# Eight modulation chunks of layer 0 move from TensorE products to VectorE dot products; attention weighs its values one head later

## The reference

```python
mod_l = split((silu(c) @ ada_w[i] + ada_b[i])[:, None, :], N_MOD)      # 6 rows of 1024
mod_c = split((silu(c_ctx) @ ada_w[i] + ada_b[i])[None, None, :], N_MOD)
a_l = modulate(rms_norm(x, norm1_w[i]), mod_l[0], mod_l[1])            # x * (1 + scale) + shift
...
q, k, v = project(a)            # low-rank latents, RMS norms, rotary part; 8 heads
o_l = softmax(q_l @ k_all.T * scale) @ v_all ; o_c = softmax(q_c @ k_c.T * scale) @ v_c
x = x + mod_l[2] * (o_l @ w_o)
x = x + mod_l[5] * swiglu(modulate(rms_norm(x, norm2_w[i]), mod_l[3], mod_l[4]), w1, w3, w2)
```

## Time and profile before

| | |
|---|---|
| median of three runs | 2816.22 us |
| profiled execution, its own time | 2820.6 us |
| its span | 2818.8 us |
| PE busy | 2587.3 us (92%) |
| PEld busy | 1440.2 us (51%) |
| DVE busy | 1079.4 us (38%) |
| ACT busy | 650.4 us (23%) |
| mean granted TensorE clock | 0.972 |
| DMA moved | 664.83 MB |

### The profile page before, as it was taken

How to read it: one execution, slowest core, us unless ns; L and a number is a source line. 1 busy time by engine, 2 the same in 40 slices (tenths; PEclk the granted TensorE clock), 3 DMA queues, 4 the chain that set the end, 5 groups by cost and what they waited for, 6 DMA issues and landing times. The chain is left out here.

```text
span 2818.8 us, 32353 instructions
## 1 busy us (share of the span) xinstructions
PE 2587.3 (92%) x12008; PEld 1440.2 (51%) x12008; DVE 1079.4 (38%) x2410; ACT 650.4 (23%) x1255; POOL 28.4 (1%) x34
## 2 busy tenths in 40 slices
PE   7999999999999998999989899999989999777776
PEld 3555544444477667888654533333347765222222
DVE  2432487771046665772431522222143323010112
ACT  2343200000055553100243312122122222111011
POOL 0000000000000000000000000000010000000000
PEclk9999999999999999999999999999999999888888
DMA  6133455562222212875301799999953338999997
GB/s 265 77 122 118 179 225 234 234 244 75 97 98 75 75 46 75 311 299 194 118 15 72 312 403 421 422 422 421 421 219 126 135 112 359 421 422 422 422 422 304
DMA packets 104137, 664.83 MB, mean 236 GB/s; under 512 B 12585, under 2 KB 21033, under 8 KB 27376
## 3 DMA queue, kind: packets, MB, share of 16 engines
q1 hardware_dynamic: 98720, 651.26, 58.0%
q0 software_dynamic: 3600, 6.07, 0.6%
q10 hardware_dynamic: 1728, 6.29, 0.6%
HBM read 663.27 MB, written 7.34 MB: 238 GB/s over the span
## 5 line engine op out<-in xcount | busy, mean ns | idle before, releaser
L699 PE MATMUL PB<-A,RING 128*128 128x256 f32 (+1 forms) x1440 | 454.6, 479 | 2.4 <-ACT A L570 2.4
L699 PEld LDWEIGHTS PB<-A,RING 128*128 128x128 f32 x1440 | 273.4, 190 | 184.1 <-issue 160.2
L447 DVE SCALAR_TENSOR_TENSOR WORK<-RING,MORE 128x1024 f32<-128x1024 f32 x288 | 335.5, 1221 | 20.2 <-ACT MORE L713 11.2
L510 PE MATMUL PB<-BIG,RING 128*128 (+2 forms) x928 | 310.7, 497 | 5.6 <-PEq L664 3.3
L510 PEld LDWEIGHTS PB<-BIG,RING 128*128 128x128 f32 x928 | 175.9, 190 | 139.4 <-issue 128.7
L2552 DVE TENSOR_TENSOR BIG<-BIG,PB 64x512 f32<-64x512 f32 x32 | 22.1, 690 | 352.2 <-ACT BIG L2449 352.2
L3051 DVE TENSOR_TENSOR BIG<-BIG,PB 64x512 f32<-64x512 f32 x16 | 11.0, 690 | 372.7 <-ACT BIG L2969 372.7
L585 DVE SCALAR_TENSOR_TENSOR X<-PB,MODS,X 128x256 f32<-128x256 f32 x72 | 32.5, 480 | 298.0 <-PE PB L539 297.2
L2869 PE MATMUL PB<-RING,X 128*32 128x512 f32 x384 | 100.6, 770 | 40.6 <-DMA RING<-moe_w 40.6
L718 ACT ACTIVATE RS<-PB 128x512 f32<-128x512 f32 (+1 forms) x44 | 21.6, 491 | 414.8 <-PE PB L699 414.8
L1715 PE MATMUL PB<-A,RING 128*128 128x512 f32 x224 | 98.3, 592 | 0.0
(11 more groups left out here) (495 smaller groups left out, 3881.6 us busy)
## 6 DMA issues: line engine op xcount, KB each, us to landing
RING<-moe_w SPq DMA_DIRECT2D x144, 1024.0 KB
RING<-ada_rows SPq DMA_DIRECT2D x72, 1024.0 KB
RING<-ffn_w SPq DMA_DIRECT2D x66, 1024.0 KB
SPARE<-moe_w SPq DMA_DIRECT2D x48, 1024.0 KB, 24.1
MORE<-moe_w SPq DMA_DIRECT2D x48, 1024.0 KB, 24.9
A<-moe_w SPq DMA_DIRECT2D x40, 1024.0 KB
BIG<-moe_w SPq DMA_DIRECT2D x36, 1024.0 KB, 26.6
CST<-moe_w SPq DMA_DIRECT2D x24, 1024.0 KB
```

The source lines that it names most:

```text
L447: dve_.scalar_tensor_tensor(out=JUNK[:, n % 4, :], in0=RING[:, s, b * D:(b + 1) * D], scalar=1.0, in1=WIDE[:, side // 2, w, :], op0=ALU.mu ...
L510: last = pe_.matmul(PB[:, m, 0:tp], tile(s, 2, D)[:, r, m * P:(m + 1) * P], src(2 * i + r), start=first and r == 0, stop=False)
L699: last = pe_.matmul(PB[:, 2 * s + j, x], tile(s, KD, P, j * KD * P)[:, k, :], A[:, k, x], start=k == 0, stop=k == KD - 1)
```

## The change

Layer 0's chunks 4 to 11 are no longer computed by TensorE. All are dot products on VectorE, laid out by column like those of the other layers, in four places:
- chunks 4 and 5 in the latents stage of `mla`: four DMAs into `BIG` at the block's start, four dots after each token tile's norms (the first four ahead of them). The spread vectors (`WIDE_0`, in SPARE) are loaded at the end of `opening` in place of head weights and late constants, which SP now issues in `mla`, behind those four DMAs.
- chunks 6 and 7 in the heads stage: two dots a head, between the maxima and the shares.
- chunks 8 and 9 in the attention's output product (`side_dots` with `sides=(0, 0)`).
- chunks 10 and 11 in the output product of layer 0's feed-forward, behind the 16 dots that are there; their weights go to SPARE, A and SIL, 1.5 MB issued at the end of the feed-forward and 2.5 MB at the start of the product, ahead of SP's first load there.

In the heads stage TensorE's list is now: scores of h+1, flips of h, values of h-1. ScalarE copies the flipped scores of h, then makes the exponentials of h+1, then copies the result of h-1. Two warming products stand ahead of the last head's values. In every boundary VectorE waits for its last bias sum before GAIN.

```diff
-    def opening(latent_weights, head_weights):
+    WIDE_0 = SPARE[:, 1, :].rearrange("p (w k) -> p w k", w=2)
+    DOTS = SMALL[:, 0:16].rearrange("p (j n) -> p j n", j=2)
+
+    def gate_dot(dve, of, n, source, wide, junk):
+        m, b = n % 8, len(junk)
+        if n >= b:
+            dve.wait_ge(*of("dotted", n - b + 1))
+        dve_.scalar_tensor_tensor(out=junk[n % b], in0=source, scalar=1.0, in1=wide[:, m % 2, :], op0=ALU.mult,
+                                  op1=ALU.mult, accum_out=DOTS[:, n // 8 % 2, m:m + 1]).then_inc(sig("dotted").sem, 1)
+
+    def gate_add(dve, of, n, chunk):
+        dve.wait_ge(*of("dotted", n + 1))
+        dve_.tensor_tensor(MODS[:, 0, 4 * chunk:4 * chunk + 4, :], DOTS[:, n // 8 % 2, :].rearrange("p (n w) -> p n w", w=2),
+                           ada_bias(0, 4 * chunk, 4), ALU.add).then_inc(sig("mod_added").sem, 1)
...
                     latent_weights(sp, j)
-                head_weights(sp)
-                sp.dma_start(CST[:, late:CON["decay"][0]], io["consts_late"]).then_inc(sig("late_in").sem, 16)
-                sp.dma_start(SPARE[:, 0, 0:2 * 7 * HD], io["decay"]).then_inc(sig("late_in").sem, 16)
+                sp.dma_start(WIDE_0.rearrange("p w k -> p (w k)"), io["cwide"][0]).then_inc(sig("wide_in").sem, 16)
...
             elif product:
+                if gates:
+                    for n in range(2):
+                        sp.dma_start(GATE_TILES[1 + n], ada_of(0)[10 + n, 1 - n]).then_inc(loaded[7 + n].sem, 16)
+                    sp.dma_start(GATE_TILES[4], ada_of(0)[11, 1, :, D:2 * D]).then_inc(loaded[9].sem, 16)
                 with sp.Fori(0, pairs) as i:
...
             for share in side_shares(sides):
-                side_dots(dve, of, sides, share, 0, 11)
+                side_dots(dve, of, sides, share, 0, chunks)
+            added = len(sides)
+            if gates:
...
+                for n in range(16):
+                    if n % 4 == 0:
+                        dve.wait_ge(*of(f"loaded{6 + n // 4}", 32 if n == 12 else 16))
+                    gate_dot(dve, later, n, halves[n // 2], WIDE[:, 0], [JUNK[:, b, :] for b in range(4)])
+                    if n % 8 == 7:
+                        gate_add(dve, later, n, 10 + n // 8)
+                added += 2
+            if added:
+                dve.wait_ge(*of("mod_added", added))
...
             def _(sp):
+                for n in range(4):
+                    sp.dma_start(BIG[:, n * SLOT:(n + 1) * SLOT], ada_of(0)[4 + n // 2, n % 2]).then_inc(loaded[6 + n].sem, 16)
+                mla_heads(sp)
...
-                def side_products(h):
-                    if h:
-                        pe.wait_ge(sig("mod_added").sem, sig("mod_added").at(h))
...
                 scores(0)
                 for h in range(HEADS):
+                    if h:
+                        pe.wait_ge(sig("turned").sem, sig("turned").at(2 * h))
                     if h + 1 < HEADS:
                         scores(h + 1)
                     flips(h)
-                    side_products(h)
-                    weigh(h)
-                    side_flips(h)
+                    if h:
+                        weigh(h - 1)
+                keep_warm(7, 2)
+                weigh(HEADS - 1)
...
             def _(act):
+                act.wait_ge(sig("wide_in").sem, sig("wide_in").at(16))
+                act_.activation(WIDE_0, WIDE_0, ACT.Silu).then_inc(sig("wide_silued").sem, 1)
+                act_.activation(SMALL[:, 250:251], con("eps"), ACT.Sqrt)
...
+                act.wait_ge(*of("dotted", 16))
                 for u in range(units):
...
+                dve.wait_ge(sig("wide_silued").sem, sig("wide_silued").at(1))
+                latent_dots(0)
                 for t in range(NT):
...
+                    if t < 3:
+                        latent_dots(t + 1)
...
-                    if h:
-                        dve.wait_ge(sig("mod_flipped").sem, sig("mod_flipped").at(h))
...
+                    for w in range(2):
+                        gate_dot(dve, of, n + w, RING[:, s, h % 2 * D:h % 2 * D + D], WIDE_0, HEAD_JUNK)
                     for j in range(2):
                         dve.wait_ge(sig("exped").sem, sig("exped").at(2 * h + j + 1))
```

More of the change, by code:

```diff
@@ L433, in side_shares, with side_dots @@
         return spots[:len(sides)], spots[len(sides):]
-    def side_dots(dve, of, sides, share, i, chunk):
+    def side_dots(dve, of, sides, share, i, chunks):
         dots = 8 * len(sides)
@@ L453, in side_dots @@
             if x == 1:
+                chunk = chunks[j]
                 dve_.tensor_tensor(MODS[:, side, bass.ds(4 * chunk, 4), :],
@@ L456, in side_dots, with boundary @@
                                    ada_bias(side, 4 * chunk, 4), ALU.add).then_inc(sig("mod_added").sem, 1)
-    def boundary(product, gain, layer, shift, scale, t, free, rest, sides=(), begun=False):
+    def boundary(product, gain, layer, shift, scale, t, free, rest, sides=(), begun=False, chunks=(11, 11), gates=False):
         at = {name: signal.base for name, signal in signals.items()}
@@ L614, in boundary @@
             loaded[s].passed(16)
-        passed(mod_added=len(sides), dotted=8 * len(sides))
+        passed(mod_added=len(sides) + 2 * gates, dotted=8 * (len(sides) + 2 * gates))
+        for n in range(4 if gates else 0):
+            loaded[6 + n].passed(32 if n == 3 else 16)
         for s in range(2 if product and not begun else 0):
@@ L725, in _ @@
                     for s in range(2):
[L726 removed]
+                        side_dots(dve, of, sides, shares[s], i, (i, i))
                         dve.wait_ge(sig("silu_made").sem, sig("silu_made").at(2 * i + s + 1))
@@ L808, in mla @@
         PTB = [w for w in (WORK[:, 3 * T:6 * T], AF[:, 3 * T:6 * T])]
-        ROW = WORK[:, 6 * T:8 * T].rearrange("p (b t) -> p b t", b=2)
+        HEAD_SPOTS = (3, 2, 4, 5)
+        LATENT_JUNK = [MORE[:, b * D:(b + 1) * D] for b in (2, 3)]
+        HEAD_JUNK = [RING[:, 1, b * D:(b + 1) * D] for b in range(2)]
         def latent(t):
@@ L1026, in _, with exps @@
                 unit_out(units - 1)
-                for h in range(HEADS):
+                def exps(h):
                     bank, b = 3 * (h % 2), h % 2
@@ L1060, in _, with latent_dots @@
                 chain(last)
+                def latent_dots(tile):
+                    dve.wait_ge(*of(f"loaded{6 + tile}", 16))
+                    for m in range(4):
+                        at = tile * SLOT + m // 2 * D
+                        gate_dot(dve, of, 4 * tile + m, BIG[:, at:at + D], WIDE_0, LATENT_JUNK)
+                    if tile % 2:
+                        gate_add(dve, of, 4 * tile + 3, 4 + tile // 2)
+                dve.wait_ge(sig("wide_silued").sem, sig("wide_silued").at(1))
+                latent_dots(0)
                 for t in range(NT):
@@ L1156, in mla @@
         for s in (2, 3, 4, 5):
-            used[s].passed(HEADS // 2)
-            loaded[s].passed(16 * HEADS // 2)
+            used[s].passed(1)
+            loaded[s].passed(16)
+        for n in range(4):
+            loaded[6 + n].passed(16)
         n = HEADS
```

104 lines of the change are left out of this document (61 added, 43 removed).

## The result

The changed kernel takes **2795.27 us**, the median of 6 executions (2793.55 to 2797.03), against 2815.95 for the kernel before beside it (6 executions, 2815.04 to 2818.84). The ratio is 0.9927, interval 0.9917 to 0.9937, and the gain 20.7 us. The forecast was 2794.5.

A forecast was written before the change was run, and what follows sets the result against it. TensorE's own work was taken to bound seven of eight heads. Attention's output product starting 22.2 us earlier, other places free, took 2816.2 to 2794.0; plus 0.5 for the clock gave 2794.5, eight-in-ten range 2791 to 2802.

The forecast's parts named there:

- TensorE's list bounds the heads, and what leaves it is gained: Heads stage: TensorE is busy 86.10 of 86.10 us; eight chunk products and flips, 21.4 us, leave its list.
- The replayed chain: Heads: ScalarE's copies have 1.5 us to spare, VectorE's shares 3.8; new waits only at head 2's scores and the last head.
- The head's length: Heads: 12.28 us less 2.67 for chunk products and flips leaves 9.61 us of TensorE a head, for six heads.
- The clock term: Whole kernel: 0.5 us added to 2794.0 for possible stretches at the 1.2 GHz level.
- The first rival: Heads: the clock falls at the new short waits, costing 1.7 to 3.4 us; 2796 to 2797.5 if once; chance 22%.
- One aside of the prediction: Heads: 2.8 us of the gain is the old last head's slow clock and wait, offset by new waits and warming products.
- The sum of 22.2: Attention's output product starts at 241.13 in place of 263.29, a difference of 22.2 us, taken as the whole gain.
- The dots cost nothing: Heads: two dots at a pace of 1.15 us each stay under the chain by 0.6 us, so no cost.
- The upper bound of 1.7: Heads: if dots take twice the pace, 2.3 us each, only the last head's wait grows, by 1.7 us.
- The 0.6 us to spare: Heads: VectorE's dots have been over for 0.6 us when its reciprocal is wanted, at s + 9.5.
- The latents cost nothing: Latents: 4.6 us of dots before each reciprocal fit VectorE's idle time; moved DMAs no cost, bounds 0 and +1.
- The second weight tile is in time by 1.9 us: Feed-forward's output product: 6.3 MB at 430 GB/s take 14.6 us, landing at 640.5 against 642.40 wanted; no wait.

The follow-up runs named there:

- the short ones: Changed kernel with all 64 dot products of layer 0's eight chunks cut from 1024 columns to 32; 2794.05 us, ratio 0.9917.

## Why the prediction was right

- **TensorE's list bounds the heads, and what leaves it is gained.** Right. The replayed chain held too: ScalarE's copies and VectorE's shares were in time in all heads but the first and last, with waits of 1.16 (forecast 1.27) and 1.12 (1.04). The experiment that puts the values back shows that this had to be argued: without the later values the same list takes 9.3 us more.
- **The head's length was mis-sized**, 9.61 against 9.33. The 12.28 less the chunk products and flips takes what is left of a head to be as long as before. From start to start it is shorter: flips 1.36 for 1.46, values 2.59 for 2.69 (the row at 181.00 is 1.89 long where the earlier trace rows have 1.99), scores 5.38 for 5.46, 0.28 in all. That these are hand-overs between tiles of different shape, which are gone with the 32-column products and the flips of two columns, is argued; no run changes the shapes alone. From the scores of head 2 to the last wait that is 56.3 us, not 57.7.
- **The clock term was in the wrong place.** The first rival (the clock falls at the new short waits, 22%) did not happen at either new wait. It happened at an old one, the 0.97 in front of the first scores, and cost 3.65 - 1.98 = 1.67 us, near its lower bound. The Trainium skill, "TensorE: Matmul & The Clock Gate", section "A second HAM failure mode: psum-queue depth-cycling", says that frequent short idles between product groups are enough to make the clock swing. The traces here show less regular behaviour than that: a single 0.97 was followed by slow products in two profiles, 0.97 or 0.98 at the same place by none in eight others, and 1.16 and 1.12 in the changed kernel's heads did nothing. I know of no row that tells the cases apart beforehand. The forecast's 0.5 for the clock was a mean of such cases.
- **These two errors cancel**, which is luck. Start of the stage -0.23, slow products +1.67, flips of head 0 +0.07 (1.53 for 1.46), six heads -1.36, the two waits -0.03, last head 9.34 for 9.68, -0.34: together -0.22, and the output product starts at 240.91 for 241.13. The 2795.27 hit is better than its parts. One aside of the prediction does not come out of the rows: 2.8 us is the old last head's slow clock alone, and its wait of 2.36 comes on top. The sum of 22.2 went by starts and is not touched by this.
- **The dots cost nothing.** Right, and shown by the short ones (80.42 us for 80.41). The upper bound of 1.7 was not needed. The 0.6 us to spare was 0.69. The experiments show attention only; the 32 dots in the two output products were cut short in the same run, and its median is 1.2 us below the changed kernel's, inside the spread.
- **The latents cost nothing.** Right: first tile at 48.94 (49), dots over at 53.6 (54), first scores at 158.83 (159 within one).
- **The warming products were put at 1.71.** Their length is right (235.50 to 237.22), their price is 0.75, since a wait for the single value bank stood behind them. That wait was not in the replay.
- **The second weight tile is in time by 1.9 us**: wrong, it had nothing to spare and cost 0.3. Two terms failed. The bytes took 1.0 us longer than at 430 GB/s throughout (619.1, where the forecast's 640.5 less 22.4 is 618.1): the burst moved 403 to 440 GB/s in most steps but 150 to 330 in four of them, where one group of loads ends and the next begins. And the sum ended with the last byte, while the landing, for which TensorE waits, came about 1 us behind it (619.1 and 620.1). By the 358 GB/s of the Trainium skill ("DMA: Bandwidth & Descriptors", section "Where 436 GB/s comes from") TensorE would have waited 1.1 us. A wait that short is not far from what was measured, but the steps disagree with its reason: most are over 400.
- **Not foreseen**: the 0.5 us in layer 1's feed-forward. Before, its first products wait 1.00 for ScalarE. In eight of the ten profiles of kernels with moved chunks they wait for a weight tile instead, 1.44 in the first profile of the changed kernel and 1.57 in the second, which waits another 1.01 at a later tile. Neither of the two kernels that keep the chunk products on TensorE waits for a transfer there. No run varies this, so the cause stays open. With it 21.6 and 20.2 of the 22.4 are left in these two profiles, and the medians are 20.7 apart. The opening adds to the spread: its slow stretch is 6.8 us in some profiles and 13.7 in others, about 2 us of time.

## What to carry to other kernels

When work moves from the bounding engine to another, the gain is its own time only if the chain through the other engines is shorter than what is left; replay that chain for a middle step, and again for the first and the last, which have nothing to stand in front of their waits. Here reordering alone left the median where it was and was worth some 9 us with the move, so parts are tested together as well as alone. When bytes go ahead of a load that an engine will want, count to the landing and not to the last byte moved. And find how far the cover goes: four dots a head were hidden in every middle head but cost about 5 us through the first and the last, and six set the pace and lost all 20 us.

## What the runs showed of the hardware

- A single wait of TensorE of 0.97 or 1.12 us was followed by a stretch at the 1.2 GHz level in some profiles (3.65 us for products of 1.98 behind 0.97; 1.74 for 1.09 and 3.78 for 1.98 behind 1.12, with four dots), and by none in others: eight of ten with 0.97 or 0.98 at the first scores, and 1.12 ahead of the last flips. In the two profiles with the waits filled by products that nobody needs, the clock stayed up there. That the filling did it is not shown, since it mostly stayed up without.
- A transfer landed about 1 us behind the last bytes moved: the second weight tile's burst ended at 619.1 and the tile landed at 620.1.
- A head without the 32-column products and the two-column flips is 0.28 us shorter in the parts that stay (9.33 for 9.61). Which of the changes in TensorE's list does that was not tested apart.
- A dot product of 1024 columns on VectorE runs at a pace of 1.15 us whether its source and scratch are slots of RING or lie elsewhere, beside DMA and TensorE at work.
